# The order of the three matmuls of a split product: low weights first in the row form

## The chip, the cores and the metric

The kernel runs on one core of a Trainium2 chip. The metric is the device time of one execution in microseconds (us), from several executions of the same program.

## The reference

A float32 model of two blocks on 256 tokens of width 1024. The first block has two layers; each is a feed-forward network, a mixer with three attention-like branches, and a second feed-forward network. The second block has two layers as well, each a mixer and a smaller feed-forward network. Nearly all of the arithmetic is products of activations with large weight matrices:

```python
def swiglu(x, w_in, w_out):
    gate, up = jnp.split(x @ w_in, 2, axis=-1)
    return (jax.nn.silu(gate) * up) @ w_out

proj = x @ w_in + b_in                       # mixer, 1024 x 4232
gates = jax.nn.sigmoid(x @ w_gate + b_gate)  # mixer, 1024 x 3072
...
return merged @ w_out                        # mixer, 1024 x 1024
```

## The kernel before, in words

**Split products.** Every weight and every activation that enters one of these products is held as two tiles of type float32r: a high part, which is the number rounded to that type, and a low part, which is what the rounding left. ScalarE writes the high part of a weight unit (WH, line 983) and VectorE the low part (WL, line 1364), from the raw unit RW that a DMA brought. A product x·w is then taken as three matmuls that accumulate in one PSUM bank: high·high, high·low and low·high. low·low is left out. The three are called a triple here, and `mm3` (line 461) issues one.

**Two forms.** A TensorE matmul holds one operand in the array (stationary, loaded by a weight load of its own) and streams the other (moving). In the *flipped form* (lines 463 to 465) the weights are stationary and the activations stream, so the result has output channels on the partitions. In the *row form* (lines 466 to 468) a [128 x 128] tile of activations is stationary and a slice of the weight unit, mostly [128 x 512], streams, so that the result has tokens on the partitions.

**Who uses the row form.** `rows_part` (line 486) issues it for one unit of weights (KU = 2 slices of 128 input channels) and one half t of the tokens; `kv_part` issues it for the values of one projection. The callers of `rows_part` take the weight units in groups of two, mostly, and go through the group once for each half of the tokens. Other products of the kernel have their triples written out: `seven_part` (lines 541 to 543) and `tile_part` (lines 559 to 562, gate and up projections; there a weight is stationary and the low weight's matmul comes ahead of the high weight's for all slices but the first).

**Order and waits.** All engines' programs are generated from one walk over the work, so the order on each engine is fixed. `rows_part` waits once for the whole unit, then for the activations, then, if it begins a sum, for its PSUM bank:

```python
self.wait_ge("lo", u.n)
for kk in range(u.nk):
    kt = k0 + kk
    self.wait_each(x.ready(kt, t))
    st, sp = first and kk == 0, last and kk == u.nk - 1
    for off, width, bks in parts:
        if st:
            self.emptied(bks[t])
```

The signal "lo" of a unit is raised when VectorE has written its low part, which it computes from the high part. After the last triple one semaphore update tells that the unit's slots, high and low together, can be filled again, and, at the end of a sum, that the bank is full.

Of the kernel before, what the change touches and what calls it, by code (L numbers as in the profile page):

```python
# [454 lines left out]
class TensorProgram(Program):  # L455
# [5 lines left out]
    def mm3(self, o, xh, xl, wh, wl, start, stop, flip=False):  # L461
        if flip:
            self.e.matmul(o, wh, xh, start=start, stop=False)  # L463
            self.e.matmul(o, wl, xh, start=False, stop=False)  # L464
            return self.e.matmul(o, wh, xl, start=False, stop=stop)  # L465
        self.e.matmul(o, xh, wh, start=start, stop=False)  # L466
        self.e.matmul(o, xh, wl, start=False, stop=False)  # L467
        return self.e.matmul(o, xl, wh, start=False, stop=stop)  # L468

    def vectors(self, g, b):  # L470
# [3072 lines left out]
```

## Time and profile before

| what | value |
|---|---|
| median of 3 runs | 2285.76 us (2285.3 to 2287.43) |
| span of the profiled execution, first to last instruction | 2283.4 us |
| time of the profiled execution beside its span | not listed on its own; the span is 2.4 us under the median |
| PE (TensorE matmul) busy | 2250.3 us, 99% of the span, 14127 instructions |
| VectorE / ScalarE / GpSimd busy | 71% / 52% / 6% |
| mean granted TensorE clock | 0.997 |

PE is the matmul side of TensorE, PEld its weight loads, which overlap the matmuls. A matmul's record is longer than the time by which it delays the next, since matmuls are pipelined: the distance from one start to the next is the cost, the record's duration is not.

### The profile page before, as it was taken

The page shows a single profiled execution, that of the slowest core. Times are in us where ns is not written, and L with a number is a line of the kernel's source. Part 1 is how long each engine was busy: PE and PEld are TensorE (multiplying, and loading weights), DVE is VectorE, ACT ScalarE, POOL GpSimd, SP SyncE. Part 2 cuts the span into 40 slices and gives each one's busy share as a digit, 9 for nine tenths or more (in the row PEclk, how much of TensorE's full clock was granted, in tenths as well). Part 3 has the DMA queues.
Part 4 walks back from the last instruction along what each step waited for, and adds up shares of the span by engine and source line. Part 5 has one row for each costly group of instructions (what it writes and reads, how often), then busy time and mean ns, then how long its engine had stood idle before and what let it go on. Part 6 is the DMA issues. An engine that isn't in the chain of part 4 may idle for free.

```text
span 2283.4 us, 34563 instructions
## 1 busy us (share of the span) xinstructions
PE 2250.3 (99%) x14127; PEld 1927.4 (84%) x14127; DVE 1624.1 (71%) x2491; ACT 1193.1 (52%) x1872; POOL 128.4 (6%) x185
## 2 busy tenths in 40 slices
PE   8999999999999999999999999999999999989999
PEld 7888899888888888888898877888878888867887
DVE  5777768857777777768668667776877778666776
ACT  5555446534555546555356444655444555545553
POOL 2100010120000000000100110000000000420000
PEclk9999999999999999999999999999999999999999
DMA  6765564435565556655554336665644666643654
GB/s 225 224 190 192 189 222 122 140 121 177 192 191 190 183 193 203 190 191 198 191 183 139 127 115 209 199 192 173 212 161 166 207 191 194 196 130 104 200 179 148
DMA packets 283567, 408.17 MB, mean 179 GB/s; under 512 B 13700, under 2 KB 170688, under 8 KB 283152
## 3 DMA queue, kind: packets, MB, share of 16 engines
q1 hardware_dynamic: 275600, 380.91, 51.9%
q0 software_dynamic: 7808, 25.04, 3.8%
q8 instruction: 112, 1.84, 0.3%
q14 instruction: 47, 0.39, 0.1%
HBM read 403.98 MB, written 1.91 MB: 178 GB/s over the span
## 4 chain that ended last, share of the span: by engine, by line
PE 89%; DVE 7%; ACT 3%; issue 1%; DMA 1%; SPq 0%; DVEq 0%; ACTq 0%
PE PS L560 24%; PE PS L466 12%; PE PS L468 12%; PE PS L467 12%; PE PS L559 11%; PE PS L463 2%; PE PS L465 2%; PE PS L464 2%; DVE WL L1364 2%; PE PS L562 2%; PE PS L483 1%; PE PS L543 1%; PE PS L541 1%; PE PS L542 1%; DVE QX L1659 1%
## 5 line engine op out<-in xcount | busy, mean ns | idle before, releaser
L1364 DVE TENSOR_TENSOR WL<-RW,WH 128x1024 fp32r<-128x1024 f32 x682 | 809.0, 1220 | 177.7 <-ACT WH L983 173.3
L560 PE MATMUL PS<-XT,WH 128*128 128x512 f32 x2368 | 808.0, 394 | 0.0
L983 ACT ACTIVATE WH<-RW 128x1024 fp32r<-128x1024 f32 x682 | 685.2, 1042 | 232.7 <-PE PS L468 62.9
L559 PE MATMUL PS<-XT,WL 128*128 128x256 f32 x2072 | 580.8, 280 | 0.0
L560 PEld LDWEIGHTS PS<-XT,WH 128*128 128x128 f32 x2368 | 425.2, 188 | 76.1
L559 PEld LDWEIGHTS PS<-XT,WL 128*128 128x128 f32 x2072 | 389.9, 188 | 13.4
L466 PE MATMUL PS<-WH,XT 128*128 128x512 f32 (+4 forms) x640 | 249.3, 390 | 3.8 <-DVE WL L1364 2.9
L468 PE MATMUL PS<-WH,XT 128*128 128x512 f32 (+4 forms) x640 | 240.5, 376 | 0.0
L467 PE MATMUL PS<-WL,XT 128*128 128x512 f32 (+4 forms) x640 | 240.0, 375 | 0.0
L466 PE MATMUL PS<-WH,HTH 128*128 128x512 f32 x488 | 192.6, 395 | 0.0
L468 PE MATMUL PS<-WH,HTL 128*128 128x512 f32 x488 | 192.2, 394 | 0.0
L467 PE MATMUL PS<-WL,HTH 128*128 128x512 f32 x488 | 191.4, 392 | 0.0
L463 PE MATMUL PS<-XT,WH 128*128 128x256 f32 x560 | 164.1, 293 | 2.3 <-DVE Z L1546 1.0
L464 PE MATMUL PS<-XT,WL 128*128 128x256 f32 x560 | 158.1, 282 | 0.0
L465 PE MATMUL PS<-XT,WH 128*128 128x256 f32 x560 | 158.1, 282 | 0.0
L1434 DVE TENSOR_TENSOR HM<-PS,HM 128x256 f32<-128x256 f32 x148 | 62.4, 422 | 133.1 <-ACT HM L1020 133.1
L466 PEld LDWEIGHTS PS<-WH,XT 128*128 128x128 f32 x640 | 121.2, 189 | 36.2 <-DVE XT L1375 8.6
L1020 ACT ACTIVATE HM<-PS 128x256 f32<-128x256 f32 x148 | 56.9, 384 | 169.6 <-PE PS L560 166.4
L468 PEld LDWEIGHTS PS<-WH,XT 128*128 128x128 f32 x640 | 121.1, 189 | 23.8
L467 PEld LDWEIGHTS PS<-WL,XT 128*128 128x128 f32 x640 | 121.4, 190 | 19.7
L1020 ACT ACTIVATE SG<-PS 128x256 f32<-128x256 f32 x148 | 54.2, 381 | 122.2 <-PE PS L560 120.8
L463 PEld LDWEIGHTS PS<-XT,WH 128*128 128x128 f32 x560 | 106.7, 190 | 6.9 <-issue 2.8
(500 smaller groups left out, 3221.8 us busy)
## 6 DMA issues: line engine op xcount, KB each, us to landing
RW<-in_w_ff_in SPq DMA_DIRECT2D x256, 512.0 KB, 4.4
RW<-in_w_ff_out SPq DMA_DIRECT2D x128, 512.0 KB, 4.5
RW<-in_w_in SPq DMA_DIRECT2D x56, 512.0 KB, 4.8
RW<-in_w_gate SPq DMA_DIRECT2D x48, 512.0 KB, 4.2
RW<-in_ffn_gate SPq DMA_DIRECT2D x44, 512.0 KB, 4.5
RW<-in_ffn_up SPq DMA_DIRECT2D x44, 512.0 KB, 4.7
RW<-in_ffn_down SPq DMA_DIRECT2D x44, 512.0 KB, 4.6
RW<-in_w_out SPq DMA_DIRECT2D x16, 512.0 KB, 4.8
```

The lines of the kernel that those rows point to most:

```text
L463: self.e.matmul(o, wh, xh, start=start, stop=False)
L464: self.e.matmul(o, wl, xh, start=False, stop=False)
L465: return self.e.matmul(o, wh, xl, start=False, stop=stop)
L466: self.e.matmul(o, xh, wh, start=start, stop=False)
L467: self.e.matmul(o, xh, wl, start=False, stop=False)
L468: return self.e.matmul(o, xl, wh, start=False, stop=stop)
L559: self.e.matmul(k.PS[:, b.n, 0:T], wl, k.XTH[:, kt, :], start=False, stop=False)
L560: ins = self.e.matmul(k.PS[:, b.n, :], wh, k.XT[:, kt, :], start=kt == 0, stop=kt == 7)
L983: self.e.activation(u.hi_out, raw, ACT.Copy).then_inc(*self.s["hi"].up(u.n))
L1020: self.e.activation(f[2 + part][:, n, j * T:j * T + T], self.k.PS[:, b.n, 0:T], ACT.Copy).then_inc(*self.s["ffn_a"].up((seq, sl, n, part, j)))
L1364: self.e.tensor_tensor(u.lo_out, raw, u.hi_out.bitcast(F), ALU.subtract).then_inc(*self.s["lo"].up(u.n))
L1434: self.e.tensor_tensor(v, self.k.PS[:, b.n, T:2 * T], v, ALU.add).then_inc(*self.s["ffn_v"].up((seq, sl, n, part, j)))
```

## The change

Within a triple of the row form the first two matmuls change places. The stationary operands stay in their order (high activations, high activations, low activations). The moving ones were high, low, high weights and are now low, high, high. The `start` mark, which makes the first matmul of a sum overwrite its bank, stays on the first of the three, now the one with the low weights. The flipped form, `seven_part` and `tile_part` stay as they are.

```diff
@@ -463,8 +463,8 @@
             self.e.matmul(o, wh, xh, start=start, stop=False)
             self.e.matmul(o, wl, xh, start=False, stop=False)
             return self.e.matmul(o, wh, xl, start=False, stop=stop)
-        self.e.matmul(o, xh, wh, start=start, stop=False)
-        self.e.matmul(o, xh, wl, start=False, stop=False)
+        self.e.matmul(o, xh, wl, start=start, stop=False)
+        self.e.matmul(o, xh, wh, start=False, stop=False)
         return self.e.matmul(o, xl, wh, start=False, stop=stop)
```

## Rows read from the trace of the kernel before

**Rows 1.** The page: span, and busy time of the two sides of TensorE

```profile
span 2283.4 us, 34563 instructions
PE 2250.3 (99%) x14127; PEld 1927.4 (84%) x14127; DVE 1624.1 (71%) x2491; ACT 1193.1 (52%) x1872; POOL 128.4 (6%) x185
```

**Rows 2.** The page: the chain that ended last, by engine and by line

```profile
PE 89%; DVE 7%; ACT 3%; issue 1%; DMA 1%; SPq 0%; DVEq 0%; ACTq 0%
PE PS L560 24%; PE PS L466 12%; PE PS L468 12%; PE PS L467 12%; PE PS L559 11%; PE PS L463 2%; PE PS L465 2%; PE PS L464 2%; DVE WL L1364 2%; PE PS L562 2%; PE PS L483 1%; PE PS L543 1%; PE PS L541 1%; PE PS L542 1%; DVE QX L1659 1%
```

**Rows 3.** Lines 466 to 468: count, duration ns min/median/max, first and last start

```profile
L466 PE MATMUL PS<-WH,HTH x488: 387/393/483, 193.6 to 2278.8; 128*128 128x512 f32 x163
L466 PE MATMUL PS<-XT,HTH x72: 389/389/399, 207.2 to 2262.1; 128*128 128x512 f32 x72
L466 PE MATMUL PS<-WH,Ob x32: 389/393/505, 422.7 to 1287.7; 128*128 128x512 f32 x32
...
L467 PE MATMUL PS<-WL,HTH x488: 387/392/403, 193.8 to 2279.0; 128*128 128x512 f32 x163
...
L468 PE MATMUL PS<-WH,HTL x488: 388/394/402, 194.1 to 2279.2; 128*128 128x512 f32 x163
```

**Rows 4.** Matmul groups, the first over all shapes: count, busy us, mean ns, idle

```profile
L466 PE MATMUL PS<-WH,XT 128*128 128x512 f32 (+4 forms) x640 | 249.3, 390 | 3.8 <-DVE WL L1364 2.9
...
L560 PE MATMUL PS<-XT,WH 128*128 128x512 f32 x2368 | 808.0, 394 | 0.0
...
L466 PE MATMUL PS<-WH,XT 128*128 128x512 f32 x528 | 217.7, 412 | 3.4 <-DVE WL L1364 2.9
L468 PE MATMUL PS<-WH,XT 128*128 128x512 f32 x528 | 209.0, 396 | 0.0
L467 PE MATMUL PS<-WL,XT 128*128 128x512 f32 x528 | 208.5, 395 | 0.0
...
L464 PE MATMUL PS<-XT,WL 128*128 128x256 f32 x560 | 158.1, 282 | 0.0
L465 PE MATMUL PS<-XT,WH 128*128 128x256 f32 x560 | 158.1, 282 | 0.0
```

**Rows 5.** Timeline, row form at width 512: start us, duration us

```profile
244.89 0.40 PE L466 MATMUL PS<-WH,HTH 128*128 128x512 f32 x1
245.12 0.39 PE L467 MATMUL PS<-WL,HTH 128*128 128x512 f32 x1
...
250.19 0.40 PE L468 MATMUL PS<-WH,HTL 128*128 128x512 f32 x1
```

**Rows 6.** Timeline, flipped form at width 256

```profile
294.04 0.28 PE L463 MATMUL PS<-XT,WH 128*128 128x256 f32 x1
294.16 0.28 PE L464 MATMUL PS<-XT,WL 128*128 128x256 f32 x1
...
299.79 0.28 PE L464 MATMUL PS<-XT,WL 128*128 128x256 f32 x1
299.91 0.28 PE L465 MATMUL PS<-XT,WH 128*128 128x256 f32 x1
```

**Rows 7.** Line 466, idle time before it: what ended it, us, times

```profile
  DVE XT L1375: 8.6, 19
  DVE WL L1364: 6.2, 2
  issue: 4.8, 21
  DVE SX L1566: 0.4, 2
```

**Rows 8.** Timeline around one such restart

```profile
519.82 0.50 PE L466 MATMUL PS<-WH,XT 128*128 128x512 f32 x1
...
520.15 0.39 PE L467 MATMUL PS<-WL,XT 128*128 128x512 f32 x1
```

**Rows 9.** Waits for the third matmul of a triple: us, times, longest

```profile
ACT WH L983 <- PE PS L468: 62.9, 44, 2.7
DVE X L1386 <- PE PS L468: 25.0, 12, 8.3
```

**Rows 10.** Stretches: busy us (count) PE, PEld, DVE, ACT, POOL; granted clock

```profile
2012.00:2016.00 4.00, 0.66 (x4) 0.42 (x4) 3.79 (x13) 1.11 (x2) 0.76 (x1) 0.91 0.86 264
2016.00:2020.00 4.00, 3.01 (x14) 3.01 (x15) 3.79 (x8) 1.86 (x4) 1.19 (x2) 0.50 0.29 96
2020.00:2030.00 10.00, 10.00 (x60) 8.94 (x58) 6.89 (x13) 4.33 (x15) 1.79 (x4) 0.72 1.01 268
```

## The prediction, on record before the result was known

> **What bounds the kernel now.** I read the page's busy times first, then its chain of waits, then the row form's lines by themselves, and last the timeline at two places where it runs undisturbed. The reader should see one engine that hardly ever stops. Matmuls are busy for 2250.3 of 2283.4 us [rows 1], and the chain that ended last is 89% matmuls; lines 466, 467 and 468, the three of the row form, carry 12% each [rows 2]. So TensorE's matmul stream sets the time, and what makes a matmul of the row form cheaper or dearer passes straight into it. Nothing covers it.
>
> **How much of the stream is touched.** Line 466 ran 640 + 488 + 72 times, and 32 times for each of five further inputs, of which one row stands for all: 1200 + 160 = 1360 triples, 4080 of the 14127 matmuls [rows 1, 3, 4]. A few of them are narrow: of the 640, 528 stream 512 columns [rows 4] and 112 fewer; the other 1248 are wide. What a wide one costs is the distance between starts: from 244.89 to 250.19 us stand 24 matmuls, 23 steps, 5.30 / 23 = 0.230 us [rows 5]. The wide row form thus takes about 1248 x 3 x 0.230 = 861 us, 38% of the span, in line with the chain's 36%.
>
> **The change part by part.**
>
> *Matmuls removed and added.* None. Per triple two streams of a high slice and one of a low slice stay, and the widths stay. The low slice streams no faster or slower than the high one: medians 393, 392 and 394 ns for the three positions in the largest regular group, 488 of each [rows 3], and 412, 395 and 396 ns on average in the group of 528, where the first carries the restarts [rows 4]. The sum of a triple doesn't depend on the order in which these durations are added. Cost 0.
>
> *Weight loads.* The stationary operands are the same tiles in the same order, and there is one load per matmul now (14127 and 14127 [rows 1]), also where the same activations are loaded twice running. Cost 0.
>
> *Waits.* `rows_part` waits for the unit's low part ahead of its first triple, and the low part is computed from the high one. So at the first matmul both are there, whichever goes first. No wait is added or moved, nothing queues behind a new one, and no queue of SP or GpSimd is touched. Had the wait for the low part stood between the first and second matmul, streaming it first would have cost something; it doesn't. Cost 0.
>
> *Releases.* The update that frees a unit or hands over a bank hangs on the third matmul, which is unchanged. ScalarE waits 62.9 us in all for it and VectorE 25.0 us [rows 9]; both are let go at the same distance from the triple's beginning as before. Cost 0.
>
> *The new neighbours.* This is the one thing that the trace of before doesn't show for this form: the second and third matmul now stream the same [128 x 512] slice one right after the other, while the stationary tile changes under it. The nearest rows are those of the flipped form, which does just that with its first two: line 463 and 464 both stream the high activations, 465 streams the low ones. From 294.04 to 299.91 us stand 51 matmuls, 50 steps of 0.117 us on average, and the step from a slice to the same slice is 0.12 us [rows 6]. Line 464, the repeated stream, and line 465, a changed one, have the same mean duration over 560 each, 282 ns [rows 4]. These means are given to 1 ns, so an effect of the repeat is under about 1 ns at 256 columns. Twice that for 512 columns on all 1360 triples bounds it at 2 ns x 1360 = 2.7 us on either side. I take 0, since the rows show equality. The gate and up products point the same way: there the low weight's matmul already leads and the next streams 512 columns that begin with the same 256, and its mean is 394 ns [rows 4], as in the row form.
>
> *The first matmul after a stop.* 44 times PE sat idle ahead of line 466 [rows 7], and there the first step is longer: 519.82 to 520.15 us, 0.33 in place of 0.23 [rows 8]. The first matmul would now stream the low slice. Its stationary tile is the same, so I expect the same 0.1 us and cost the edit at 0. The bounds are that all of it goes, or that it doubles: 44 x 0.10 = 4.4 us either way, both unlikely.
>
> **The sum.** 0 + 0 + 0 + 0 + 0 + 0: the profiled execution would again have a span of 2283.4 us. It stands 2.4 us (0.1%) under the median of the three runs, and I add that back: 2285.8 us. About 0.2%, 4.6 us, is what a measurement of this kernel can tell from no change; that would take 4.6 us / 1360 = 3.4 ns per triple.
>
> **A rule weighed.** The step that the rows show is 0.230 us for 512 columns [rows 5]. The Trainium skill (TensorE: Matmul & The Clock Gate, Back-to-back issue gap) gives columns / 2.4 + 2.5 ns, 216 ns here. By that figure of the Trainium skill some 14 ns of each step, an estimate of 17 us over one matmul of each of the 1248 wide triples, would be something that a kinder order might win back. The trace doesn't support that the order is what they hang on, since all three positions have them alike.
>
> **The rivals.**
>
> *A repeated slice is read slower (slower than before).* Place: the third matmul of each triple, line 468. For it: this form was never run with two equal neighbours. Against it: lines 464 and 465 agree [rows 4]. For a price I take the largest difference between positions that the rows show, 412 against 396 ns [rows 4], although restarts explain it: 16 ns x 1360 = 21.8 us, 2307.6 us. It decides from 3.4 ns per triple. Chance 0.03.
>
> *A repeated slice is read faster.* The same place with the other sign. The most that the spread of one line allows is from its median to its shortest, 394 - 388 = 6 ns [rows 3]; x 1360 = 8.2 us, so 2277.6 us. Against it again the equality of 464 and 465. Chance 0.03.
>
> *The restarts cost more or less.* As bounded above, 2281.4 or 2290.2 us if all 44 change by their whole 0.1 us. Even then the change is inside 0.2%. Chance of either 0.01, and only the sum with something else would show.
>
> *The clock.* Where PE was nearly idle, 0.66 of 4 us, the granted clock then fell to 0.50, that is 1.2 GHz, and stood at 0.72 on average for the next 10 us [rows 10]. The change opens no such gap. If it brought a second such stretch, the loss would be (1 - 0.50) x 4 + (1 - 0.72) x 10 = 4.8 us, 2290.6 us, just over the bound. Chance 0.02.
>
> *The change does nothing that the chip can see.* That is my forecast, 2285.8 us, chance 0.91.
>
> **How the numbers follow.** Within 0.2% is the forecast (0.91) and the restarts (0.01), 0.92. Faster by over 0.2% is the faster repeat, 0.03. Slower is the slower repeat (0.03) and the clock (0.02), 0.05. The range takes the forecast with the bound of the repeat, 2.7 us on either side, 2283.1 to 2288.5 us, a spread of runs as before (2285.3 to 2287.43 us) inside it. It leaves out the rivals, which together hold under 2 in 10: 2283 to 2289 us.
>
> **What would show it.** In the profile after, lines 466 and 467 swap their inputs (WL, then WH) and every position keeps a median of 392 to 394 ns; the steps in the timeline stay at 0.230 us, the one from 467 to 468 included; PE's busy time stays within a few us of 2250, counts stay at 14127, and the waits for line 468 keep their size. I am wrong if the step from 467 to 468 differs from the other two by over 3 ns, if the first steps after a stop change, or if a stretch appears in which the granted clock falls and before it didn't.

## The result, and the profile after

The changed kernel takes 2287.36 us (median of 21 runs) against 2285.39 us for the kernel before (21 runs). The ratio is 1.0013, 95% interval 1.0007 to 1.0018. This is within the 0.2% called no change in the prediction, and 1.6 us above the 2285.8 us forecast. The interval doesn't hold 1, so something small did happen, and the profile shows where. A time of a run alone could not: the unchanged kernel, run against itself below, differs by 1.1 us in its medians.

The page of the changed kernel, its span and busy times, which answer to [rows 1]:

```profile
span 2285.1 us, 34563 instructions
PE 2253.4 (99%) x14127; PEld 1929.6 (84%) x14127; DVE 1623.5 (71%) x2491; ACT 1192.8 (52%) x1872; POOL 128.5 (6%) x185
```

The counts are the same. The span is 1.7 us longer and PE is busy 2253.4 - 2250.3 = 3.1 us more: the time is in the matmuls, not in waits for others. PE's idle time (span less busy time) is 31.7 us against 33.1; the unchanged kernel, run again, has 32.6, so 0.5 of those 1.4 us comes without any change. The matmul groups by shape of the changed kernel (count, busy us, mean ns, idle before), which answer to [rows 4]:

```profile
L560 PE MATMUL PS<-XT,WH 128*128 128x512 f32 x2368 | 808.0, 395 | 0.0
...
L466 PE MATMUL PS<-WL,XT 128*128 128x512 f32 x528 | 218.0, 413 | 3.3 <-DVE WL L1364 2.9
L468 PE MATMUL PS<-WH,XT 128*128 128x512 f32 x528 | 210.0, 398 | 0.0
L467 PE MATMUL PS<-WH,XT 128*128 128x512 f32 x528 | 209.0, 396 | 0.0
...
L465 PE MATMUL PS<-XT,WH 128*128 128x256 f32 x560 | 158.3, 283 | 0.0
L464 PE MATMUL PS<-XT,WL 128*128 128x256 f32 x560 | 158.3, 283 | 0.0
```

The inputs of 466 and 467 have changed places. In this group of the row form the three lines gained 0.3, 0.5 and 1.0 us; the flipped form's lines 464 and 465 0.2 us each, and the gate and up products' line 560 nothing. Their line 559 gained 0.8 us (580.8 to 581.6), but stands at 580.8 again in another kernel with the changed order (moved by 256 bytes, below). So the growth is the row form's, 1 or 2 ns for each matmul, and largest in line 468. The timeline of the changed kernel, over the same 24 matmuls as [rows 5]:

```profile
244.87 0.39 PE L466 MATMUL PS<-WL,HTH 128*128 128x512 f32 x1
245.10 0.40 PE L467 MATMUL PS<-WH,HTH 128*128 128x512 f32 x1
...
250.22 0.40 PE L468 MATMUL PS<-WH,HTL 128*128 128x512 f32 x1
```

23 steps in 5.35 us, 0.2326 us each, where there were 0.2304. One sign that the prediction named did fail: not every position keeps a median of 392 to 394 ns. The third matmul's, 394 ns in [rows 3], is 397 now:

```profile
L468 PE MATMUL PS<-WH,HTL x488: 387/397/406, 193.8 to 2281.0; 128*128 128x512 f32 x163
```

The other views are nearly as they were. Waits for line 468 in the changed kernel (us, times, longest), to compare with [rows 9]:

```profile
ACT WH L983 <- PE PS L468: 63.0, 44, 2.7
DVE X L1386 <- PE PS L468: 26.3, 13, 7.9
```

And the stretch in which the clock falls, in the changed kernel (busy us and counts of PE, PEld, DVE, ACT, POOL, then the granted clock), to compare with [rows 10]:

```profile
2012.00:2016.00 4.00, 1.82 (x15) 1.62 (x16) 2.71 (x9) 2.13 (x6) 0.76 (x1) 1.00 0.46 153
2016.00:2020.00 4.00, 1.76 (x11) 1.52 (x10) 3.83 (x9) 0.84 (x2) 0.00 (x0) 0.73 0.55 185
2020.00:2030.00 10.00, 10.00 (x51) 9.16 (x51) 7.22 (x13) 5.03 (x13) 2.38 (x4) 0.60 0.88 220
```

The same dip lies about 2 us later: (1 - 0.73) x 4 + (1 - 0.60) x 10 = 5.1 us lost. Before it was 4.8 us in the last two rows and (1 - 0.91) x 4 = 0.4 us in the first, 5.2 in all. Both kernels also have one short dip near 1690 us (mean granted clock 0.93 from 1680 to 1705 us in each). So the clock has no part in the difference.

### The profile page after: what moved, and what is told of

Read it like the earlier page. It is cut to its first block, busy times and chain, and to the rows that moved or that the text cites. A ratio compares the mean times of both kernels' runs of the same rounds, so it can differ in the third digit from the quotient of the medians.

```text
span 2285.1 us, 34563 instructions
## 1 busy us (share of the span) xinstructions
PE 2253.4 (99%) x14127; PEld 1929.6 (84%) x14127; DVE 1623.5 (71%) x2491; ACT 1192.8 (52%) x1872; POOL 128.5 (6%) x185
## 4 chain that ended last, share of the span: by engine, by line
PE 89%; DVE 7%; ACT 3%; issue 1%; DMA 1%; SPq 0%; DVEq 0%; ACTq 0%
PE PS L560 24%; PE PS L466 12%; PE PS L468 12%; PE PS L467 12%; PE PS L559 11%; PE PS L463 2%; PE PS L464 2%; PE PS L465 2%; DVE WL L1364 2%; PE PS L562 2%; PE PS L483 1%; PE PS L543 1%; PE PS L541 1%; PE PS L542 1%; DVE QX L1659 1%
## 5 line engine op out<-in xcount | busy, mean ns | idle before, releaser
L560 PE MATMUL PS<-XT,WH 128*128 128x512 f32 x2368 | 808.0, 395 | 0.0
L559 PE MATMUL PS<-XT,WL 128*128 128x256 f32 x2072 | 581.6, 281 | 0.0
L466 PE MATMUL PS<-WL,XT 128*128 128x512 f32 (+4 forms) x640 | 249.6, 390 | 3.6 <-DVE WL L1364 2.9
L468 PE MATMUL PS<-WH,XT 128*128 128x512 f32 (+4 forms) x640 | 241.5, 377 | 0.0
L467 PE MATMUL PS<-WH,XT 128*128 128x512 f32 (+4 forms) x640 | 240.5, 376 | 0.0
```

The lines of the kernel that those rows point to most:

```text
L466: self.e.matmul(o, xh, wl, start=start, stop=False)
L467: self.e.matmul(o, xh, wh, start=False, stop=False)
L559: self.e.matmul(k.PS[:, b.n, 0:T], wl, k.XTH[:, kt, :], start=False, stop=False)
L560: ins = self.e.matmul(k.PS[:, b.n, :], wh, k.XT[:, kt, :], start=kt == 0, stop=kt == 7)
```

## The steps, position by position

A page gives durations to 1 ns, and the effect is about that size. So the steps were also worked out from the trace's start times. A step is the time from the start of one 512-column matmul of the row form to the start of the next matmul; after the third matmul, only where the next is the first 512-column one of another triple. Its mean is taken by position; steps of 300 ns or more (restarts) are left out. Some 1130, 1240 and 1092 steps stand behind the three numbers. Single steps differ by more than any effect here, from about 225 to 240 ns; only the means are so steady. In this table and below, "distance" is how far each low-weight tile lies from its high tile, modulo 256 bytes. In the kernels before and after the distance is 6 slots x 2 slices x 520 x 4 = 24960 bytes, 97 x 256 + 128. That holds for the six main slots. For parts of its work the kernel also keeps weights in two slots inside XT, with a distance of 4096 bytes (0 modulo 256), and in two more slots in the scratch, with 4160 bytes (64); no edit below changes these distances.

```
kernel            order of streams  distance  1st>2nd  2nd>3rd  3rd>next  sum (ns)  PE busy (us)
before            high, low, high   128       232.1    230.0    231.6     693.7     2250.3
null              high, low, high   128       232.1    230.1    231.6     693.7     2251.1
pad256_before     high, low, high   128       232.0    230.1    231.6     693.7     2251.1
pad512_before     high, low, high   128       232.1    230.1    231.6     693.8     2250.8
pad1024_before    high, low, high   128       232.1    230.1    231.6     693.8     2251.0
pad2048_before    high, low, high   128       232.1    230.1    231.6     693.8     2248.5
pad4096_before    high, low, high   128       232.0    230.1    231.6     693.7     2250.6
after             low, high, high   128       231.6    230.9    233.6     696.1     2253.4
pad256_after      low, high, high   128       231.6    231.0    233.6     696.2     2254.1
pad512_after      low, high, high   128       231.5    231.0    233.6     696.1     2253.0
pad4096_after     low, high, high   128       231.6    230.9    233.6     696.1     2253.8
hhl               high, high, low   128       231.6    231.3    231.1     694.0     2251.5
pad_before        high, low, high   0         232.7    232.0    232.5     697.2     2258.9
pad_after         low, high, high   0         232.7    231.9    232.3     696.9     2258.0
```

A triple of the changed kernel costs 696.1 - 693.7 = 2.4 ns more. Over 1248 wide triples that is 3.0 us, PE's 3.1. The sum is what counts: a matmul that starts late makes the step before it longer and its own shorter, so a single position tells less.

## The experiments

**The kernel before against itself.** No edit.

> The kernel before once more, unchanged, timed against itself. If the measured 0.13% of the change is noise of the comparison, this control can come out as far off: 0.999 to 1.0015, and PE's busy time can differ from 2250.3 us by as much as the 3.1 us that the changed kernel showed. If the difference is real, the ratio is 1.000 within 0.0005 and PE's busy time returns within 0.5 us.

2286.28 us against 2285.18, ratio 1.0003 (0.9995 to 1.0012). This is the same kernel, and the medians are 1.1 us apart. Its page, the busy times:

```profile
PE 2251.1 (99%) x14127; PEld 1927.9 (84%) x14127; DVE 1623.9 (71%) x2491; ACT 1193.1 (52%) x1872; POOL 128.6 (6%) x185
```

PE busy came back within 0.8 us (0.5 was expected, a miss) and every mean step within 0.1 ns. One by one, 95% of the row form's steps are within 1 ns of the same step in the first trace; between the kernels before and after it is 26%. The step is the sharp instrument; the time of a run is not, for an effect of 2 us.

**A repeated slice with the low weights last.** This tells a cost of the repeat from a cost of what surrounds it. The edit is shown against the kernel before; the stationary operands move too and are now low, high, high activations.

```diff
-        self.e.matmul(o, xh, wh, start=start, stop=False)
-        self.e.matmul(o, xh, wl, start=False, stop=False)
-        return self.e.matmul(o, xl, wh, start=False, stop=stop)
+        self.e.matmul(o, xl, wh, start=start, stop=False)
+        self.e.matmul(o, xh, wh, start=False, stop=False)
+        return self.e.matmul(o, xh, wl, start=False, stop=stop)
```

> Row form in the order low activations x high weights, high x high, high x low: the same slice is streamed twice running, but the low weights come last in place of first. Theory A (a repeated slice costs something): as the changed kernel, ratio 1.001 to 1.002, PE busy 2252.5 to 2254. Theory B (what costs is that the low slice follows the high slice of the triple before, at the boundary between triples): like before, 0.9995 to 1.0005, PE busy 2250 to 2251. Theory C (each pairing of addresses gets its own few ns): anything within 0.2%, not foretold by the order, and steps that shift by 1 to 3 ns at single positions.

2284.76 us, ratio 0.9995 (0.9986 to 1.0004). The matmul groups of this kernel:

```profile
L466 PE MATMUL PS<-WH,HTL 128*128 128x512 f32 x488 | 192.7, 395 | 0.0
L467 PE MATMUL PS<-WH,HTH 128*128 128x512 f32 x488 | 192.1, 394 | 0.0
L468 PE MATMUL PS<-WL,HTH 128*128 128x512 f32 x488 | 191.9, 393 | 0.0
```

The slice is streamed twice running here too, and the step between the two is 231.6 ns, no longer than the first step of the kernel before (232.1). A triple costs 694.0 ns, 0.3 over before and 2.1 under the change. PE busy is 2251.5 us. Theory A falls: it asked for 2252.5 at least. Theory B (the boundary from high to low) is nearly right at this placement, 0.5 us over its upper bound of 2251; theory C isn't excluded.

**The low tiles moved by 3712 bytes, both orders.** The move makes the distance 24960 + 3712 = 28672 bytes, 112 x 256. Unused tiles ahead of and behind the low ones keep everything else at one place in both kernels: what lies ahead of the low tiles, the high tiles and XT among it, doesn't move, and what lies behind them moves by 4096 bytes.

```diff
+        sb("PAD0", [P, 928])
         self.WL = [sb(f"WL{n}", [P, KU, UW], R) for n in range(SPL)]
+        sb("PAD1", [P, 96])
```

> The order of before; the low-weight tiles are moved up by 3712 bytes per partition, so that each stands a multiple of 4096 bytes from its high tile, in place of 384 bytes beyond one; everything behind them moves by 4096 bytes. Theories A and B: order alone decides, so ratio 1.000 and PE busy 2250 to 2251. Theory C (placement): PE busy moves by over 1 us either way, since the pairing of the addresses changes, by the steps of lines 466 and 467 above all.

> The changed order, low weights first, with the same move of the low-weight tiles by 3712 bytes. Theories A and B: the difference to before stays, ratio 1.001 to 1.002 and PE busy 2 to 3.5 us over the moved kernel with the old order. Theory C: the difference between the two orders changes by over 1 us or turns its sign, and the step from line 468 to 466, 2 ns longer than before in the changed kernel, loses that.

Old order: 2292.47 us, ratio to the kernel before 1.0032 (1.0020 to 1.0044). Low weights first: 2292.26 us, 1.0028 (1.0019 to 1.0037). The groups of the moved kernel with the old order (its line numbers are two higher, so 468 to 470 are the row form, 562 the gate and up products):

```profile
L562 PE MATMUL PS<-XT,WH 128*128 128x512 f32 x2368 | 810.1, 395 | 0.0
...
L468 PE MATMUL PS<-WH,XT 128*128 128x512 f32 x528 | 218.3, 413 | 3.4 <-DVE WL L1366 2.9
L470 PE MATMUL PS<-WH,XT 128*128 128x512 f32 x528 | 209.8, 397 | 0.0
L469 PE MATMUL PS<-WL,XT 128*128 128x512 f32 x528 | 209.5, 397 | 0.0
```

And of the moved kernel with the low weights first:

```profile
L562 PE MATMUL PS<-XT,WH 128*128 128x512 f32 x2368 | 810.1, 395 | 0.0
...
L468 PE MATMUL PS<-WL,XT 128*128 128x512 f32 x528 | 218.3, 413 | 3.4 <-DVE WL L1366 2.9
L470 PE MATMUL PS<-WH,XT 128*128 128x512 f32 x528 | 209.7, 397 | 0.0
L469 PE MATMUL PS<-WH,XT 128*128 128x512 f32 x528 | 209.6, 397 | 0.0
```

The reader is to see two things. The two orders are alike to 0.1 us a line: the changed order's cost is gone, and it stands 0.3 ns a triple under the old one. And a line that no edit of any order touches, 562, the gate and up products, rose from 808.0 to 810.1 us, though its own operands, high weights and activations, didn't move. What moved is the low weight of its neighbour, line 561: the mean step from 562 to 561 rose from 231.4 to 232.8 ns (1776 steps). There the low weight is stationary, so the placement of a loaded operand counts and not only that of a streamed one.

The pages of the two, old order first:

```profile
PE 2258.9 (99%) x14127; PEld 1929.3 (84%) x14127; DVE 1624.0 (71%) x2491; ACT 1192.7 (52%) x1872; POOL 128.5 (6%) x185
```

```profile
PE 2258.0 (99%) x14127; PEld 1928.7 (84%) x14127; DVE 1624.2 (71%) x2491; ACT 1193.4 (52%) x1872; POOL 128.4 (6%) x185
```

PE busy is 2258.9 us in the old order and 2258.0 with the low weights first, 8.6 and 7.7 us over the kernel before. The short dip of the clock near 1690 us is deeper in the first (mean 0.86 over the 25 us from 1680 to 1705, against 0.93 in the second and before), which is 1.7 us of its 8.6. Theories A and B foretold 2 to 3.5 us more for the changed order here; it is 0.9 us less, and the dip accounts for that. Theory C foretold that the difference would change by over 1 us or turn its sign, and that the long third step would go; both came. The steps of the two moved kernels even agree one by one: 85% are within 1 ns of each other, as many as between the changed kernel and its repetition moved by 256 bytes (84%). That is what one would expect if only addresses modulo 256 count, since high and low tiles then look alike.

**The move by 4096 bytes, both orders.** The control: the same shift of the scratch behind the low tiles, with the distance again 128 modulo 256.

```diff
+        sb("PAD0", [P, 1024])
         self.WL = [sb(f"WL{n}", [P, KU, UW], R) for n in range(SPL)]
```

> The order of before; the low-weight tiles and everything behind them are moved up by 4096 bytes, so that each low tile stands 384 bytes beyond a multiple of 4096 from its high tile, as in the kernel before. If the placement counts modulo 4096 bytes (or a divisor of it), PE busy is again 2250 to 2251.5 us and the ratio 1.000 within 0.001. If the 0.3% of the first padded kernels came from anything else that padding brings (the scratch moved, another distance), it is again 2258 us and 1.003.

> The changed order with the move of 4096 bytes. If the placement counts modulo 4096 bytes, the difference between the orders is back: PE busy 2253 to 2254.5 us, and the mean step from the third matmul of a triple to the next first one is 2 ns longer than in the kernel with the old order and the same move. If the 0.13% was chance, both orders agree here.

Old order 2286.08 us, 1.0009 (0.9999 to 1.0018); low weights first 2287.49 us, 1.0014 (1.0004 to 1.0024). The intervals of the two overlap. The steps don't leave it open: all three positions of each order are back at their values to 0.1 ns, and PE busy is 2250.6 and 2253.8 us. So neither padding nor the shifted scratch made the 7 us of the pair above.

**How far the period goes down.** The old order with moves of 1024 and 2048 bytes, one run each, the tile behind shrunk so that together they make 4096:

```diff
+        sb("PAD0", [P, 256])    # 512 for the move by 2048 bytes
         self.WL = [sb(f"WL{n}", [P, KU, UW], R) for n in range(SPL)]
+        sb("PAD1", [P, 768])    # 512
```

> The order of before; the low tiles stand 384 + 1024 = 1408 bytes beyond a multiple of 4096 from their high tiles. Theory C (placement) says a PE busy time of its own, between 2247 and 2260 us and not the 2250.3 of before; a theory that only the order or only equal distances count says 2250 to 2251.

> The order of before; the low tiles stand 384 + 2048 = 2432 bytes beyond a multiple of 4096 from their high tiles. If the placement counts modulo 2048 bytes already, PE busy is 2250 to 2251.5 us as before; if modulo 4096, another value, over 1 us off.

2285.5 and 2282.04 us in their one run each. The steps are those of before, and so theory C as I had put it, a busy time of its own for 1408 bytes, missed for the first: 1024 bytes is already a period. PE busy of the second, 2248.5 us, lies 2 us under its sisters while its row-form steps are the same. Most of that is the clock: this execution has no dip near 1690 us, where the others have one (mean granted clock from 1687 to 1692 us 1.00, against 0.66 before), and (1 - 0.66) x 5 = 1.7 us.

**Moves of 256 and 512 bytes, both orders.** The same edit with 64 and 960, and with 128 and 896 elements.

> The order of before; the low tiles stand 384 + 256 = 640 bytes beyond a multiple of 1024 from their high tiles. Moves by 1024, 2048 and 4096 bytes left every mean step within 0.1 ns. Theory C (placement, modulo 1024 bytes or less) gives this kernel a PE busy time of its own, 2248 to 2259 us; the theory that only coinciding low and high tiles cost (distance 0) says 2250 to 2251.5 us.

> The changed order at a distance of 640 bytes modulo 1024. If the change is slower by its order, PE busy is 2 to 3.5 us over the kernel with the old order at the same distance, as at 384 bytes. If the two orders only meet other pairs of addresses, the difference is another one: between -3 and +3 us, and its sign is open.

> The order of before; distance 384 + 512 = 896 bytes modulo 1024. If the placement counts modulo 512 bytes, PE busy is 2250 to 2251.5 us and the three mean steps are those of before within 0.1 ns; if only modulo 1024, they are others.

> The changed order at a distance of 896 bytes modulo 1024. Modulo 512: PE busy 2253 to 2254.5 us, as the changed kernel, with the step from the third matmul to the next first one 2 ns longer. Modulo 1024 alone: a difference of its own, of either sign.

By 256 bytes: old order 2285.49 us, 0.9994 (0.9981 to 1.0007); low first 2288.45 us, 1.0014 (1.0004 to 1.0023). By 512 bytes: 2285.47 us, 1.0005 (0.9995 to 1.0014), and 2288.52 us, 1.0020 (1.0010 to 1.0029). The page of the kernel moved by 256 bytes with the old order:

```profile
PE 2251.1 (99%) x14127; PEld 1928.0 (84%) x14127; DVE 1623.7 (71%) x2491; ACT 1193.2 (52%) x1872; POOL 128.8 (6%) x185
```

And with the low weights first:

```profile
PE 2254.1 (98%) x14127; PEld 1927.4 (84%) x14127; DVE 1623.1 (71%) x2491; ACT 1192.6 (52%) x1872; POOL 126.8 (6%) x185
```

Neither move changed a step. I had expected a cost of its own at 640 bytes and was wrong again: with 256 bytes as the period, 640 and 896 are both the old 128, and these four kernels repeat the comparison of the change twice. Together: seven kernels with the old order at a distance of 128 have PE busy for 2250.5 us on average (2248.5 to 2251.1), four with the low weights first 2253.6 us (2253.0 to 2254.1). The two sets don't touch.

## Why the prediction was right, and where it was off

*What bounds the kernel* held: 3.1 us more in the matmul stream came out as 1.97 us in the medians, 3.0 us by the ratio and 1.7 us in the span. "Nothing covers it" isn't shown to the last microsecond: PE's idle time is 1.4 us shorter, and how much of that is the change's can't be told.

*Matmuls removed and added, cost 0*: this is the step that was off. I argued that the sum of a triple doesn't depend on the order in which its three durations are added. It does, by 2.4 ns of 694, because what a step costs hangs on which tile comes after which. I had read that from medians of 393, 392 and 394 ns, given to 1 ns, and took their nearness for indifference.

*The new neighbours, 0 with bounds of 2.7 us on either side*: the term that was mis-sized. The step from the second to the third matmul, between the two equal slices, grew by 0.9 ns, about 1.1 us in all; the first step shrank by 0.5 ns. The largest part, 2.0 ns, came at the boundary, from the third matmul to the next triple's first, which I hadn't priced: it used to lead from a high slice to the next high slice and now leads to a low one. I looked only at the repeat, since it was the conspicuous thing, and the low-last experiment shows that a repeat is not what costs. The flipped form, my nearest row, was no witness for that boundary, for there the low weights are stationary and not streamed. That the median stayed inside the range is in part luck: the bounds of 2.7 us covered the repeat alone, and the whole came to 3.0.

*Weight loads, waits, releases, restarts, cost 0*: nothing contradicts it. Loads are 14127, ScalarE's waits for line 468 63.0 us against 62.9, VectorE's 26.3 against 25.0. The restarts were counted too low, though: I took the 44 idle times, but the first step is 300 ns or more in 114 wide triples, most of them behind a transpose or a small matmul with no idle time between. The bound would have been 114 x 0.10 = 11 us and not 4.4. These first steps add up to 38.3 us in both kernels. The idle times ahead of line 466 in the changed kernel have the same three main entries as [rows 7]:

```profile
  DVE XT L1375: 8.6, 19
  DVE WL L1364: 6.2, 2
  issue: 4.8, 21
```

*The rivals.* The slower repeat was right in its sign and wrong in its place, and stayed under its deciding point, 2.4 ns a triple against 3.4. The faster repeat and the clock didn't occur. Nothing in the rows of before told the sign. A hint that placement counts was there, and I passed over it: see the row with XT below.

*The rule weighed* promised up to 17 us, an estimate from the figure in the Trainium skill (TensorE: Matmul & The Clock Gate, Back-to-back issue gap). The same section of the Trainium skill gives that figure for an isolated matmul and about 131 ns for 512 columns in a stream; no step here is near 131. No order tried brought a mean over all wide triples under 230.0 ns. But one placement that the kernel already has does. In 72 triples the weights lie in the slots inside XT, and these rows of the kernel before belong beside those of [rows 3]:

```profile
L467 PE MATMUL PS<-XT,HTH x72: 387/389/396, 207.4 to 2262.3; 128*128 128x512 f32 x72
L468 PE MATMUL PS<-XT,HTL x72: 389/389/397, 207.6 to 2262.6; 128*128 128x512 f32 x72
```

The mean steps there are 228.6, 226.8 and 227.4 ns, 682.7 a triple. After the first steps of a run of such triples they settle: steps 13 to 22 of the five unbroken runs of eight triples have a mean of 226.6 to 226.7 ns in all fourteen traces, whatever the order and the move of the low tiles. That is 680 ns a triple, 13 to 14 under the kernel before. Once settled, the order costs nothing there; over all 72 triples the changed kernel needs 685.6 ns, and the difference lies in the first steps, right behind matmuls from the main slots. By that difference, the 1176 other wide triples would hold an estimated 16 us. No run here moved the main slots to find out.

**The cause, as far as it is shown.** The cost of a step depends on where the low tiles lie modulo 256 bytes. Shown: moves of them by five multiples of 256 bytes leave all positions alone (by 256, 512 and 4096 bytes in both orders, by 1024 and 2048 in the old one), a move by 14.5 times 256 changes all of them, and the steps of the gate and up products too, and there the two orders cost the same. The new order is dearer at the placement the kernel happens to have.

Not shown: which quantity it is. The edits move the low tiles against the high ones, against the activations and against a fixed grid of 256 bytes all at once, so "distance" in the table is a label and not the cause. A distance of 0 by itself isn't what makes steps dear: it is also that of the slots inside XT, which have the cheapest steps of all. These differ from the main slots in one more thing: their slices all start at one place modulo 256, while in a main slot the second slice starts 2080 bytes (32 modulo 256) behind the first, and the next slot 4160 bytes (64) behind. Nor is it shown which pair of reads meets. It isn't one pair of neighbours alone: where a run of XT triples begins, steps of up to 237 ns go on for one to ten matmuls before the 226.7 is reached, though every operand streamed is already in XT. The weight load of the next stationary tile runs while a slice streams, so it may be these two, or the end of one stream and the beginning of the next. No other move than by half of 256 bytes was tried off the period; whether one beats both kernels is open. Low weights last cost 0.3 ns a triple more than the kernel before, so no version here beats it.

## What to carry to other kernels

In a kernel that is bound by an unbroken stream of matmuls, an order that adds and removes nothing can still be worth 1 to 3 ns for each matmul, which thousands of them turn into microseconds; the mean distance of starts, taken by position in the pattern, shows it where a run's time hardly does. Before crediting an order with such a gain, move the operands, here by half of 256 bytes, and look whether the gain stays. Compare the same form across the places where its tiles lie, too: here one place gave 680 ns where the others gave 694. A neutral edit that shifts tile addresses is not neutral below about 0.3%, so compare variants at equal addresses.

## What the runs showed of the hardware that wasn't expected

Moving six weight tiles by 3712 bytes made the kernel 0.32% slower (1.0020 to 1.0044), with the same instructions in the same order; moving them by 4096 bytes instead gave 1.0009 (0.9999 to 1.0018) with unchanged steps. Matmuls of one shape and form settle at 226.7 ns a step with weights in XT and average 231.2 ns over all wide triples. And mean steps over a thousand matmuls repeat from trace to trace to 0.1 ns, while the runs' times spread over 8 us.
